# Sums of the late modulation moved into the projection stage, and the inverses of a recurrence spread over four corners of the array

## The reference

```
first block:
  shift, scale, gate = split(silu(c) @ w_ada + b_ada)        # modulation, 3 x 2048 outputs
  h = rmsnorm(x) * (1 + scale) + shift                       # the same for ctx
  u = h @ w_in                                               # projection, 4096+32 and 3456+1024 columns
  ya = gdn_mixer(u[:, :4128])                                # 8 heads of 128, gated delta rule, both directions
  yb = rwkv_mixer(u[:, 4128:])                               # 16 heads of 64, RWKV-7 scan, both directions
  x = rmsnorm(x + gate * (concat(ya, yb) @ w_out))
second block:
  shift, scale, gate = split(silu(c_2) @ w_ada_2 + b_ada_2)
  attention and convolution on x * (1 + scale) + shift; x = layer_norm(ALPHA * x + gate * y)
```

## Time and profile before

| what | value |
|---|---|
| median of three runs | 3387.04 us |
| the profiled execution | 3392.42 us |
| its span | 3390.7 us |
| PE busy | 2961.2 us, 87% of the span |
| DVE busy | 1998.7 us, 59% |
| ACT busy | 1032.4 us, 30% |
| POOL busy | 712.0 us, 21% |
| mean granted TensorE clock | 0.946 |
| sums of the late modulation on DVE (L2572) | 240 x 747 ns = 179.2 us |

### The profile page before, as it was taken

The page is one execution under the profiler, slowest core; times in us unless marked ns, Lnnn a source line. Parts: engine busy times, 40 slices in busy tenths (PEclk is TensorE's granted clock), DMA queues, the critical chain, the costliest instruction groups (busy, mean ns, idle before and its releaser), DMA issues. The chain is left out here.

```text
span 3390.7 us, 71127 instructions
## 1 busy us (share of the span) xinstructions
PE 2961.2 (87%) x30422; PEld 2485.3 (73%) x30422; DVE 1998.7 (59%) x3450; ACT 1032.4 (30%) x1668; POOL 712.0 (21%) x526
## 2 busy tenths in 40 slices
PE   5999999989999938788878688878979999998896
PEld 2688888868888737777777687766867778785484
DVE  5465465555555426677776557863242999996223
ACT  3345465443333302222222123321023444413102
POOL 0000000000000002222222100007853344473383
PEclk8999999989999969999999679998989999999998
DMA  9424434435545445555565334417332222221331
GB/s 395 170 75 149 132 117 149 134 118 167 180 154 187 126 128 176 174 179 180 178 188 181 105 121 126 131 56 265 95 120 84 81 81 75 81 93 44 130 99 68
DMA packets 265224, 465.80 MB, mean 137 GB/s; under 512 B 108224, under 2 KB 156576, under 8 KB 258544
## 3 DMA queue, kind: packets, MB, share of 16 engines
q1 hardware_dynamic: 213152, 364.71, 33.0%
q0 software_dynamic: 20672, 67.27, 6.2%
q10 hardware_dynamic: 31120, 29.72, 2.8%
HBM read 382.60 MB, written 81.63 MB: 137 GB/s over the span
## 5 line engine op out<-in xcount | busy, mean ns | idle before, releaser
L1152 PE MATMUL pjl<-high,w_high 128*128 128x512 f32 x816 | 324.5, 398 | 29.2 <-DVE low L2792 16.4
L1154 PE MATMUL pjl<-high,w_low 128*128 128x512 f32 x816 | 319.9, 392 | 0.0
L1153 PE MATMUL pjl<-low,w_high 128*128 128x512 f32 x816 | 319.7, 392 | 0.0
L3220 DVE SCALAR_TENSOR_TENSOR arena<-arena,par 128x512 f32<-128x512 f32 x232 | 293.0, 1263 | 6.8
L2188 POOL DMA_DIRECT2D arena_r<-in_w_ada x256 | 137.5, 538 | 570.1 <-DVE arena_r L2572 476.1
L1135 POOL TENSOR_TENSOR w_low<-ring_o,w_high 128x1024 fp32r<-128x1024 f32 x88 | 226.8, 2577 | 6.9
L2862 POOL TENSOR_TENSOR w_low<-ring_o,w_high 128x1024 fp32r<-128x1024 f32 x64 | 169.3, 2646 | 250.1 <-ACT w_high L3049 249.7
L1133 POOL TENSOR_TENSOR w_high<-ring_o,cst 128x1024 fp32r<-128x1024 f32 x88 | 174.0, 1977 | 213.5 <-PE pjl L1154 66.0
L1283 DVE TENSOR_TENSOR wl_in<-ring,wh_in 128x1024 fp32r<-128x1024 f32 x136 | 164.1, 1220 | 86.5 <-ACT wh_in L1276 86.4
L1264 PE MATMUL xu<-h_high,wh_in 128*128 128x512 f32 x512 | 207.9, 406 | 0.0
L1152 PEld LDWEIGHTS pjl<-high,w_high 128*128 128x128 f32 x816 | 154.6, 189 | 72.6 <-issue 27.0
(11 more groups left out here) (508 smaller groups left out, 7015.5 us busy)
## 6 DMA issues: line engine op xcount, KB each, us to landing
ring<-in_w_lr SPq DMA_DIRECT2D x136, 512.0 KB, 4.3
arena_r<-in_w_ada POOLq DMA_DIRECT2D x256, 256.0 KB, 3.8
arena_p<-in_w_ada SPq DMA_DIRECT2D x32, 1024.0 KB, 8.5
ring_o<-in_w_out SPq DMA_DIRECT2D x64, 512.0 KB, 3.7
ring_o<-in_w SPq DMA_DIRECT2D x64, 512.0 KB, 3.7
arena_r<-rk_d SPq DMA_DIRECT2D x47, 384.0 KB, 5.0
rk_d<-arena_p SPq DMA_DIRECT2D x72, 192.0 KB, 1.9
arena_p<-gate_rows SPq DMA_DIRECT2D x32, 386.0 KB, 6.2
```

Of the source, the lines that this page charges most:

```text
L1152: pe.matmul(lat, wh[:, c], ah, start=kk == 0, stop=False)
L1153: pe.matmul(lat, wh[:, c], al, start=False, stop=False)
L1154: last = pe.matmul(lat, wl[:, c], ah, start=False, stop=kk == KT - 1)
L3220: link(dve.scalar_tensor_tensor(ca[:], x[:, o:o + LAT], w[:, o:o + 1], ca[:], ALU.mult, ALU.add))
```

## The change

Four edits:

- The sums of the late modulation leave the RWKV stage for the projection stage. Two buffers instead of four hold the pieces. POOL loads piece x once piece x - 2 is used. DVE's `later(n)` is called 6, 6 and 4 pieces at a time in `front`, 16 pieces in each of the eight pair periods and 16 in each of the next seven heads. There is one accumulator; after each 16 pieces PE sums it over the partitions (`late_columns`, four products) and DVE keeps the result (`late_kept`). The 64 products of `rest` are gone.
- `values_in` and `VX` are gone; `turn_values` turns each head's values with its own 64x64 product, 12 instead of 6.
- PE's pair periods are written out instead of looped.
- In the RWKV stage `products`, `turn_back`, `left` and `right` issue both directions together: direction 0 on the diagonal corners, direction 1 on the other two, with its input and output halves crossed. One wait for both directions stands in front; the copies wait for both. The loads of the inverted blocks cross the halves of direction 1 and become eight instead of four (`inverse_in_crossed`).

The diff below is cut. Its hunks come in this order: `front_vector`; `inverse_in_crossed`; the buffers; `late_reads` and `late_columns`; POOL's list; `turn_values`; on PE `head`, `period` and the loop over the pairs; on DVE `next_head`, `head`, `period` and `later`; and, of the RWKV stage, `turn_back` (`products`, `left` and `right` are changed in the same way) and the `later` that is gone there.

```diff
-    def front_vector(dve, weights, link):
+    def front_vector(dve, weights, link, later):
...
             mods(2)
             parts(2)
+            later(6)
             weights(6)
             row(6)
+            later(6)
             weights(7)
             row(7)
+            later(4)
             mods(3)
...
+def inverse_in_crossed(eng, e, S, q, a, Z):
+
+    eng.wait_ge(S[q + "_h3"], 32 * a + 32)
+    for k in range(4):
+        for d in range(2):
+            g = (2 * k + 4 * d) % 8
+            eng.dma_start(Z[32 * k:32 * k + 32, d],
+                          e["zb_d"][6 * d:6 * d + 6, g:g + 2].rearrange("u g (i j) -> (g i) u j", j=16)).then_inc(S[q + "_h4"], 16)
...
-    VX = carve(6, P)
+    late, acc = carve(2, 512), carve(512)
...
+    def late_reads(pool, x0, x1):
+
+        for x in range(x0, x1):
+            if x >= 2:
+                pool.wait_ge(S["p_lu"], x - 1)
+            pool.dma_start(late[:, x % 2], io["w_ada"][8 + x // 16, :, x % 16]).then_inc(S[f"p_la{x % 2}"], 16)
+
+    def late_columns(pe, cols, due):
+
+        pe.wait_ge(S["p_lu"], due)
+        for c in range(4):
+            last = pe.matmul(cols[:, c:c + 1], acc[:, c * P:c * P + P], ones[:, 0:1], start=True, stop=True)
+        last.then_inc(S["p_lr"], 1)
...
+            late_reads(pool, 0, 16)
             front_pool(pool)
+            late_reads(pool, 16, 256)
...
-                pe.wait_ge(S["p_vx"], i * 4 + 2 * n + 2)
+                pe.wait_ge(S["p_mv"], i + 1)
                 for c in range(6):
-                    last = pe.matmul(ctxs[0][:, 64 * c:64 * c + 64], VX[:, c], istk, start=True, stop=True)
-                last.then_inc(S["p_vt"], 1)
+                    at = 384 * n + 64 * c
+                    last = [pe.matmul(ctxs[0][hs, 64 * c:64 * c + 64], v[hs, at:at + 64], istk[hs], start=True, stop=True)
+                            for hs in (slice(0, 64), slice(64, P))]
+                for ins in last:
+                    ins.then_inc(S["p_vt"], 1)
...
                 turn_norms(h + 1)
+                late_columns(pe, head_cols, 16 * h + 160)
                 tile(t, 3, False, (1,))
...
                 pe.wait_ge(S["p_rk"], i + 1)
+                late_columns(pe, pair_cols, i * 16 + 32)
                 pe.matmul(up[0][:, 0:LAT], blk, kds, start=True, stop=True).then_inc(S["p_bs"], 1)
...
-            with pe.Fori(0, PAIRS - 1) as i:
-                period(i, False)
-            period(PAIRS - 1, True)
+            for i in range(PAIRS):
+                period(i, i == PAIRS - 1)
...
                 head_conv(h, 0)
+                if h:
+                    later(2)
                 head_silu(h, 0)
                 if h:
                     weights(m + 6)
                 head_conv(h, 1)
                 if h:
+                    later(2)
                     weights(m + 7)
+                    later(2)
                 head_silu(h, 1)
...
                 if more:
                     weights(m + 2)
+                    later(3)
                     weights(m + 3)
+                    later(3)
...
                 if more:
                     weights(m + 4)
+                    later(2)
                     weights(m + 5)
+                    later(2)
                     next_head(h + 1, m)
...
                 sums(i, 0)
+                later(2)
                 weights(m + 2)
+                later(1)
                 weights(m + 3)
+                later(2)
                 streams(i, 0)
+                later(1)
...
                 weights(m + 4)
+                later(2)
                 weights(m + 5)
+                later(2)
                 sums(i, 1)
+                later(3)
                 weights(m + 6)
+                later(3)
                 streams(i, 1)
...
+            def later(n):
+
+                for x in range(x_[0], min(x_[0] + n, 256)):
+                    m, k = x // 16, x % 16
+                    which = 0 if m < 4 else 2
+                    c = csk[:, 3 * k + which:3 * k + which + 1]
+                    dve.wait_ge(S[f"p_la{x % 2}"], x // 2 * 16 + 16)
+                    if k == 0:
+                        if m:
+                            dve.wait_ge(S["p_lr"], m)
+                        dve.tensor_scalar(acc, late[:, x % 2], c, None, ALU.mult).then_inc(S["p_lu"], 1)
+                    else:
+                        dve.wait_ge(S["p_lu"], x)
+                        dve.scalar_tensor_tensor(acc, late[:, x % 2], c, acc, ALU.mult, ALU.add).then_inc(S["p_lu"], 1)
+                x_[0] += n
...
+    TILES4 = [(d, hs, HEADS[h ^ d]) for d in range(2) for h, hs in enumerate(HEADS)]
...
-                for d in range(2):
-                    pe.wait_ge(S["r_t"], a * NT + l * 2 + d + 1)
-                    for u in range(UN):
-                        last = [pe.matmul(o[hs, d, u], T[hs, d, u] if l else TT[a % 2][hs, d, u], istk[hs], start=True, stop=True)
-                                for hs in HEADS]
-                    done(last, "r_tr")
+                pe.wait_ge(S["r_t"], a * NT + l * 2 + 2)
+                for u in range(UN):
+                    if l:
+                        last = [pe.matmul(o[hs, d, u], T[to, d, u], istk[to], start=True, stop=True) for d, hs, to in TILES4]
+                    else:
+                        last = [pe.matmul(o[to, d, u], TT[a % 2][hs, d, u], istk[hs], start=True, stop=True) for d, hs, to in TILES4]
+                done(last, "r_tr")
...
-                    later(m, 3 * j)
```

More of the change, by code:

```diff
@@ L851, in rest @@
                     heads_out()
[L852 to L857, removed]
             for m in range(GH):
@@ L1334, in phase_proj @@
     eps = carve(1)
+    late, acc = carve(2, 512), carve(512)
+    csk, gate, mod2 = (e[k] for k in ("csk", "gate", "mod2"))
+    front_cols, pair_cols, head_cols = tp8[:, 1, 5, 0:4], tp8[:, 1, 7, 0:4], tp8[:, 0, 0, 0:4]
     sq, nr = cs, gn
@@ L1616, in _ @@
             columns()
+            late_columns(pe, front_cols, 16)
             logits_turned()
@@ L1668, in exponents @@
                 act.activation(sg, sg, ACT.Exp, scale=-EXPM).then_inc(S["p_ex"], 1)
-            def values_in(i, n):
-                act.wait_ge(S["p_mv"], i + 1)
-                for h in range(2):
-                    act.activation(diag(VX, h), chunked(v, h)[:, 6 * n:6 * n + 6], ACT.Copy).then_inc(S["p_vx"], 1)
             def values_out(i, n):
-                act.wait_ge(S["p_vt"], i * 2 + n + 1)
+                act.wait_ge(S["p_vt"], i * 4 + 2 * n + 2)
                 act.activation(V[:, 384 * n:384 * n + 384], ctxs[0][:, 0:384], ACT.Copy).then_inc(S["p_vc"], 1)
@@ L1769, in period @@
                 values_out(i, 0)
-                values_in(i, 1)
                 weights(n + 2)
@@ L1804, in period @@
                 scaled(i + 1, 2)
-                values_in(i + 1, 0)
                 weights(n + 9)
@@ L1851, in _ @@
             scaled(0, 2)
-            values_in(0, 0)
             weights(17)
@@ L2021, in period, with late_kept @@
                     next_head(0, m)
-            columns, softplus, cumulated, products_of, kept = front_vector(dve, weights, link)
+            x_ = [0]
+            def later(n):
[12 more added lines that the diff above has]
+                x_[0] += n
+            def late_kept(m):
+                cols = front_cols if m == 0 else pair_cols if m <= PAIRS else head_cols
+                dve.wait_ge(S["p_lr"], m + 1)
+                if m < 4:
+                    b = pr("b_ada", 96).rearrange("p (n s) -> p n s", s=2)[:, 32 + 4 * m:36 + 4 * m, 0]
+                    dve.tensor_tensor(gate[:, 4 * m:4 * m + 4], cols, b, ALU.add).then_inc(S["p_ld"], 1)
+                else:
+                    k = slice(4 * m - 16, 4 * m - 12)
+                    dve.tensor_tensor(mod2[:, k], cols, pr("b_ada2", 48)[:, k], ALU.add).then_inc(S["p_ld"], 1)
+            columns, softplus, cumulated, products_of, kept = front_vector(dve, weights, link, later)
             def tables():
@@ L2184, in _ @@
                 pool.memset(unused[:, n:n + 1], 0.0).then_inc(S[name], 1)
-            for x in range(256):
-                if x >= LATE:
-                    pool.wait_ge(S["r_lu"], x - LATE + 1)
-                pool.dma_start(late[:, x % LATE], io["w_ada"][8 + x // 16, :, x % 16]).then_inc(S[f"r_lw{x % LATE}"], 16)
         @block.sync
@@ L2589, in scan @@
                     fill(3 * j + 2)
-                    later(m, 3 * j + 2)
             def heads_out(i, n):
@@ L3372, in constants @@
     add("incl", np.stack([r[:, None] <= r[None], r[:, None] >= r[None]], 1))
-    lm = np.zeros((P, 3, 2, 64))
-    for lv in range(4, 7):
-        b = 1 << lv
-        for d in range(2):
-            c = np.arange(64)
-            pair = c // b
-            lm[:, lv - 4, d] = -1.0 * (r[:, None] // b == (2 * pair + 1 - d)[None])
-    add("lmask", lm)
     ch = np.arange(3456)
```

86 lines of the change are left out of this document (29 added, 57 removed).

## The result

The change makes the kernel slower: 3567.72 us median of four runs (3566.39 to 3580.24) against 3388.26 us (3385.12 to 3396.82), a ratio of 1.0534, interval 1.0503 to 1.0564. Forecast were 3472 us, in a range of 3365 to 3560. The sign was right; the forecast growth of 85 us is half of what came.

A forecast was written before the change was run, and what follows sets the result against it. PE was taken to bound the projection, PE and DVE the RWKV stage. Front +15, pairs +69, last pair +17, heads +84, RWKV stage -84, delta start -16 gave +85: 3477 us, as median 3472, range 3365 to 3560.

The forecast's parts named there:

- the stores: Projection's pairs and heads: stores only start later (7.1 us behind the first streams), their length staying the same.
- the clock: Projection: PE's clock falls after a wait, costing 2.0 us a period, taken between 1.6 and 3.6.
- the way through memory: RWKV stage, last block store to spread, about 10.5 us: eight loads instead of four change nothing, within 2 us a step.
- What one piece costs: Projection: 0.75 us of DVE, plus buffer turnaround R, 3.6 us in pairs, 3.9 in heads; groups around splits last 2R + 2.25 or 2R + 4.2.
- The last pair, +17: Projection's last pair: no slack, so all 17.3 us of the bonus product's delay count.
- Pairs and heads, +69 and +84: Projection: PE waits for late DVE work, seven pairs at 9.8 us and seven heads at 12 us longer.
- RWKV stage, -84: RWKV stage: 15 steps save 5.6 us each, 2.8 in each of two stretches, merged four-corner groups taking 0.70 us.
- rival (1): RWKV stage: the four corners take turns, a merged group stays at 1.40 us; 3521 to 3534 us, chance 0.22.
- 0 (between -2 us and +2 us a step): RWKV stage, last block store to spread: the extra loads' cost, with PE's and DVE's savings there hidden.
- Delta stage, -16: Start of the delta stage: 128 records of L856 go, saving 16 us, between 5 and 27.
- (3): Rival: projection waits fall where nobody waits, so it costs 33 us; needs landing of about 2.5 us; 3320 us, chance 0.16.
- (2): Rival: loads land in 2.6 to 2.9 us beside the projection's traffic; 3390 to 3405 us, chance 0.09.
- (4): Rival: loads land over 4.4 us in the projection; time above 3560 us, chance 0.03.

The follow-up runs named there:

- run 3: Changed kernel with all 256 sums on DVE at their places, but only the first two pieces loaded, so results are wrong: 3352.56 us, ratio 0.9915.
- run 10: Late pieces almost all single, crossed corners, eight loads on two queues, then three places mended (head's stores, pair's sum over partitions, front): 3362.09 us, ratio 0.9914.
- run 11: Changed kernel with unread 128x128 products in front of PE's two waits, 90 in each pair and 100 in each head: 3650.01 us.
- run 1: Changed kernel with the late sums back in the RWKV stage; crossed corners, turn_values and written-out periods stay: 3378.84 us, ratio 0.9989 to the kernel before.
- run 5: Changed kernel with four of the eight loads of inverted blocks issued from POOL instead of SP: 3543.96 us.
- run 2: Changed kernel with the inverses as before, on diagonal corners with four loads; late sums stay in the projection: 3549.8 us.
- runs 9 and 10 against 8: Two crossed-corner, two-queue kernels with almost all late pieces single (3389.24 us; with three places mended 3362.09) against one with bunches in DVE's long waits (3412.11).
- runs 7 to 10: Changed kernel with late pieces moved: bunches in DVE's waits, diagonal corners 3419.74 us; crossed, two queues 3412.11; almost all single 3389.24; three places mended 3362.09.

## Why the prediction was wrong, step by step

Two steps of the projection's sum failed, the stores and the clock, and one of the RWKV stage's, the way through memory. Of the 81 us by which the projection was forecast too short, the stores are 40 and the clock with the sums over partitions 28, by the cuts; the rest is spread over small terms.

**What one piece costs** was right. The loads landed in 3.2 us in the pairs and 3.8 in the heads (3.3 and 3.6 taken), and the groups lasted about what the formulas say: over the eight pairs "2, split, 1, split, 2" took 8.3 to 11.6 us, in the mean 9.9 (9.45 taken), and "3, split, 3" 10.7 to 12.0, in the mean 11.4 (11.4). `mods(3)` came at 158.2 (157.8). The last pair, +17, measured +18.

**Pairs and heads, +69 and +84, measured about +110 and +119.** Two terms failed, each in seven pairs and in seven heads. First, "`streams(i, 0)` ends 7.1 later, so do its store and ACT's gate" and "the four pieces behind `q_pre` ... cost nothing": I moved the stores in time and took their length to stay. The gate came 3.1 us later behind the streams, the first tap 2.6. The cause is the loads' traffic beside the stores: run 3, without loads, has 10.8 us to the gate (10.2 before, 13.3 changed) and 10.2 to the first convolution (10.7, 13.3). The last store in front of the gate was issued at these times, and the gate of the earlier trace rows and of the period above starts when it has landed, 1.9 us later before (452.61) and 4.5 us later in the changed kernel (527.09):

```profile
450.69 0.33 SPq L1422 DMA_DIRECT2D rx_d<-arena_p  x1
```
```profile
522.61 0.45 SPq L1428 DMA_DIRECT2D rx_d<-arena_p  x1
```

From issue to landing this store took, as the median of the eight pairs, 1.9 us before, 4.5 in the changed kernel, 2.2 without loads (run 3) and 4.2 in run 10.

Second, the clock, 2.0 a period by choice between 1.6 and 3.6, with 0.5 for `late_columns`, together 2.5: it is 4.4 in the pairs and 4.6 in the heads, of which 3.4 to 3.5 come back at full clock (run 11) and 0.95 is `late_columns` at full clock. The upper end, from the longer idle time, was the nearer row: the waits came out at 11 to 13 us and not at 7 to 9. PE after such a wait:

```profile
472.72 1.63 PE L1381 MATMUL tp<-cst,arena_p 128*128 128x1 f32 x7
474.22 2.06 PE L1616 MATMUL tp<-arena_p,cst 128*128 128x512 f32 x2
```

The bonus product took 2.06 us where it took 1.02. These two terms are 3.1 + 1.9 of the pair's 5.9 us of error (the other 0.9 is the first group of pieces) and 2.6 + 2.1 of the head's 5.0. `turn_values` and the written-out loop give nothing where PE waits, as said. But the prediction also said that they give back 1.1 us a pair where it doesn't, and that was wrong: in run 1 PE waits for nobody in the pairs, and the pair takes 65.1 us as before. Why is open.

**RWKV stage, -84, measured -56 for the 15 steps.** The one thing I doubted was right: at full clock a merged group goes twice as fast. 46 records of a group now start within 0.69 us (0.91 less the last one's own 0.22), where 48 took 1.40. But the two groups behind the spread, of eight in a step, ran at half clock, after PE had waited for the eight loads:

```profile
1643.49 1.56 PE L2333 MATMUL tp<-cst,arena_r 64*64 64x64 f32 x48 [5.04 <-DVE arena_r L2567]
...
1656.42 0.91 PE L2331 MATMUL tp<-cst,arena_r 64*64 64x64 f32 x46
```

Over the half scans those two groups have a median of 26 ns from record to record in the changed kernel and 15 in run 5, where the wait is short; the other merged groups have 15 to 16 in both. So rival (1) does not hold. By the rule of the Trainium skill ("TensorE: Matmul & The Clock Gate", section "Wait — 56ns, not 53.3ns?") starts of small products are never under about 25 ns apart; the trace's records on four corners disagree, at 0.69 us over 45 distances, 15 ns. (A product is two records here, so whole products start 31 ns apart.) What failed is "0 (between -2 us and +2 us a step)" for the way through memory, and that the other stretches' gains would come from the corners. By the table of run 2 the first two stretches gave 2.5 + 2.3 where 2.8 + 2.8 were forecast, but 1.2 + 1.9 of that is DVE's relief; in the third the relief gave 1.9 and the four extra loads took 3.0. The two hide each other: the stretch grew by only 1.1 us, so the prediction's own sign of being wrong there (longer by more than 2 us) did not show. Run 5, with two queues, comes to 5.8 us a half scan, near the forecast 5.6, but that is luck: 5.1 of it are DVE's relief (run 2), and only 0.7 are the corners.

**Delta stage, -16, measured -22** (2104 to the end, so with whatever else moved behind the scans); L856 is gone.

**Rivals.** (3), in which 8.25 us of bare sums fit into 10.1 of slack, is what run 3 shows as soon as no load is waited for; its price of +33 us to the scan measured +41. Its condition did not hold. Neither did that of (2), since no group of loads had a median landing under 3.2 us. The time is one that only (4) gave, above 3560, but not by its cause: in the pairs and heads the loads did not land later than 4.4 us in the median.

## What to carry to other kernels

What a piece of spare work costs is not its busy time but its buffer's turnaround. With two buffers, pieces that stand singly, each with two gaps in front, did better than bunches in the engine's idle time (runs 9 and 10 against 8), and both did better than pieces between a split and the engine that waits for it; which place gave how much was not tried apart. When loads are added to a stage, price what they do to the stores that someone waits for, and count how many loads a crossed layout adds to a chain that is all latency. A wait has a second price behind it, the half clock. And test the two halves of a combined edit apart: here the whole gain of the RWKV stage came from what was taken out of it, while the corners, twice as fast at full clock, lost more than they won to four more loads. Last, count what one instruction is in the trace before you size a filler by it: two records a product made the 90 products of run 11 twice as long as meant.

## What the runs showed of the hardware

Products on four corners of the array, with crossed halves, run side by side: 15 ns from record to record at full clock (26 at half clock) against 29 on two. Each small load that SP issues adds 0.5 to 0.6 us (5.1 us for eight of 12 KB, 3.0 for four; four of 24 KB took 2.7 before), and issuing half of them from POOL took 2.6 us off the third stretch. After a wait of 11 to 13 us PE loses 3.4 to 3.5 us to half clock. Sixteen loads of 256 KB in a pair period of 81 us took the store that the gate waits for from 1.9 to 4.5 us. What stays open: runs 7 to 10 never came under 3350 us, and most of what is left is in the heads; the landing of the weights in the pairs went from 4.0 us before to 5.2 in run 10, and whether that costs anything in the heads was not tried apart.
